# A hybrid RG-LRU / RWKV-7 / PEER layer on one core: norms, LRU chain, picking stage and last rows cut in halves, with more buffers and another order of the one-hot loads

## The reference

```python
h = rms_norm(x, norm1_g)
proj = h @ w_in                                   # 2048 -> LRU branch, gate branch, RWKV columns
# group A: RG-LRU, 1024 channels
a  = exp(-8 * sigmoid(xc @ wa + ba) * softplus(-lam))
bx = sqrt(1 - a * a) * (sigmoid(xc @ wi + bi) * xc)
h_t = a_t * h_(t-1) + bx_t                        # a scan over the 256 tokens
y_lru = h * gelu(gate)
# group B: RWKV-7 time mixing, 16 heads of 64 -> y_rwkv
x = x + concat(y_lru, y_rwkv) @ w_out
# PEER: 8 heads, 128 x 128 single-neuron experts, top 16 of each head
h = rms_norm(x, norm2_g)
q = h @ wq;  scores against 2 x 128 keys;  experts e = 128 * i + j;  g = softmax(best 16)
act = gelu(h . u_tab[e])                          # 128 experts (8 heads x 16) per token
x = x + sum_e  g_e * act_e * v_tab[e]
return rms_norm(x, normf_g)
```

## Time and profile before

| | before |
|---|---|
| median of three executions | 2071.92 us |
| profiled execution | 2072.16 us |
| its span | 2070.4 us |
| mean granted TensorE clock | 0.991 |
| TensorE busy | 1990.3 us (96%) |
| VectorE busy | 1546.8 us (75%) |
| ScalarE busy | 970.3 us (47%) |
| GpSimd busy | 500.9 us (24%) |
| moved by DMA | 462.00 MB, mean 223 GB/s |

### The profile page before, as it was taken

How to read it: one execution, slowest core, us unless ns; L and a number is a source line. 1 busy time by engine, 2 the same in 40 slices (tenths; PEclk the granted TensorE clock), 3 DMA queues, 4 the chain that set the end, 5 groups by cost and what they waited for, 6 DMA issues and landing times.

```text
span 2070.4 us, 35268 instructions
## 1 busy us (share of the span) xinstructions
PE 1990.3 (96%) x14048; PEld 1766.5 (85%) x14048; DVE 1546.8 (75%) x2341; ACT 970.3 (47%) x1332; POOL 500.9 (24%) x513
## 2 busy tenths in 40 slices
PE   7999999898999999999999999998989999999997
PEld 7988888786789888888888888888878888888886
DVE  5647474756453799997867888757778998989998
ACT  5434342436353444444444444445664444444443
POOL 1000000000000000000012222104665766666664
PEclk9999999999999999999999999999999999999999
DMA  7523232224555565656668888866879999999996
GB/s 251 163 73 121 65 123 73 83 89 165 179 189 173 175 187 189 184 186 190 184 223 280 283 289 285 265 192 209 281 232 315 340 341 341 347 349 361 355 353 246
DMA packets 148675, 462.00 MB, mean 223 GB/s; under 512 B 19856, under 2 KB 44480, under 8 KB 147744
## 3 DMA queue, kind: packets, MB, share of 16 engines
q1 hardware_dynamic: 114624, 338.74, 50.4%
q0 software_dynamic: 33888, 121.01, 16.7%
HBM read 430.24 MB, written 29.43 MB: 222 GB/s over the span
## 4 chain that ended last, share of the span: by engine, by line
PE 86%; DVE 6%; DMA 3%; ACT 2%; issue 1%; POOL 0%; DVEq 0%; SPq 0%; POOLq 0%; ACTq 0%
PE ps L1565 86%; DMA oneJ<-oneJ_spill 2%; DVE lo L999 1%; DVE L L1188 1%; ACT hi L658 0%; DVE xc L1007 0%; DMA x_sb<-in_x 0%; DMA vraw<-in_peer_v 0%; ACT x_sq L671 0%; ACT xr_sq L671 0%; DMA got<-in_peer_v,row_ids 0%; ACT lt L831 0%; DVE ps L1485 0%; PE ps L1714 0%; DVE xr L1007 0%
## 5 line engine op out<-in xcount | busy, mean ns | idle before, releaser
L1565 PE MATMUL ps<-hT,hi 128*128 128x512 f32 (+1 forms) x3936 | 1072.6, 345 | 6.3 <-DVE rkv L1007 3.6
L1565 PE MATMUL ps<-hT,lo 128*128 128x256 f32 x2992 | 839.2, 280 | 0.0
L1565 PEld LDWEIGHTS ps<-hT,hi 128*128 128x128 f32 x3936 | 679.8, 190 | 105.2 <-DVE rkv L1007 4.2
L999 DVE TENSOR_TENSOR lo<-raw,hi 128x1024 fp32r<-128x1024 f32 x406 | 492.3, 1224 | 230.6 <-ACT hi L658 224.3
L658 ACT ACTIVATE hi<-raw 128x1024 fp32r<-128x1024 f32 x406 | 424.4, 1059 | 450.2 <-DMA raw<-in_peer_u 371.0
L1565 PEld LDWEIGHTS ps<-hT,lo 128*128 128x128 f32 x2992 | 567.6, 190 | 0.0
L616 POOL DMA_INDIRECT got<-in_peer_v,row_ids x256 | 325.7, 1272 | 174.7 <-DVE sums L1007 116.9
L903 ACT ACTIVATE vhi<-vraw 128x1024 fp32r<-128x1024 f32 (+1 forms) x256 | 202.6, 816 | 272.1 <-DMA vraw<-in_peer_v 267.2
L1467 DVE TENSOR_TENSOR vlo<-vraw,vhi 128x1024 fp32r<-128x1024 f32 (+1 forms) x256 | 240.4, 940 | 52.6 <-ACT vhi L903 45.2
L1565 PE MATMUL ps<-vhi,a_hi 128*128 128x512 f32 (+1 forms) x768 | 252.6, 383 | 2.2 <-ACT wT L930 2.2
L1565 PE MATMUL ps<-vlo,a_hi 128*128 128x512 f32 (+1 forms) x768 | 253.5, 384 | 0.0
(11 more groups left out here) (286 smaller groups left out, 1840.5 us busy)
## 6 DMA issues: line engine op xcount, KB each, us to landing
raw<-in_peer_u SPq DMA_DIRECT2D x256, 512.0 KB, 3.6
vraw<-in_peer_v SPq DMA_DIRECT2D x128, 512.0 KB, 6.3
raw<-in_w_in SPq DMA_DIRECT2D x86, 512.0 KB, 3.6
vraw<-in_peer_v SPq DMA_DIRECT2D x128, 224.0 KB, 6.1
raw<-in_w_out SPq DMA_DIRECT2D x32, 512.0 KB, 3.5
raw<-in_wq SPq DMA_DIRECT2D x32, 512.0 KB, 3.5
oneJ_spill<-madeJ POOLq DMA_DIRECT2D x64, 256.0 KB, 5.0
oneJ<-oneJ_spill SPq DMA_DIRECT2D x64, 256.0 KB, 4.4
```

The costliest lines, as they stand in the source:

```text
L999: V.tensor_tensor(lo[n % NR][:, :], raw[n % NR][:, :], hi[n % NR][:, :].bitcast(F32), ALU.subtract).then_inc(lo_done, 1)
L1565: return nc.tensor.matmul(o, lhsT, rhs, start=start, stop=stop, skip_group_check=True)
```

## The change

It touches five places and leaves the products and their operands as they are.

- First norm: x comes in four loads (t and half of the columns), and VectorE and ScalarE square one half each of every t. Root, reciprocal and diagonal are made for one t at a time. SP also asks for `ident` and `cols`; GpSimd's other constants wait for the first projected piece.
- LRU chain: every full-tile step becomes two half-tile steps (`lru_part`, four channel blocks each), with the `hi`/`lo` pieces of w_out placed between the halves by `hi_out` and `lo_out`.
- Second norm: the last w_out tile is done for t=0 and then for t=1 by TensorE, and the adds (`add_rows`) and norms (`norm_rows`) follow per t.
- Picking stage: S_LAG from 8 to 6; four `oneG` buffers; the gelu and the weight product for two steps at a time; `load_one_j` stands in front of `load_one_i` in each step; the one-hots of VectorE stand in front of `chosen`, and the first four are made before the stage; the last scores are put in place in two parts (`LAST_TOKENS`); the eight early v loads are spread, one in every six steps (`V_FIRST, V_EVERY = 10, 6`).
- Last rows: the running sums start from the columns of x2 that a load brings (`sums_in`), not from a memset; `picked` is done twice at six places; per t there are an add, a sum, a root and a scaling, of which ScalarE takes a part (`scaled_early`), and the last v tile ends t=0 first.

The diff, cut to its core (the instruction lists of ScalarE at the LRU chain mirror those of VectorE):

```diff
-S_LAG = 8
+S_LAG = 6
 BC_TOK = 8
 N_BC = SEQ // BC_TOK
 N_GATHER = 6
 V_RAWS, V_HIS = 4, 3
-V_FIRST = 44
-N_ONEJ, N_ONEI = 4, 10
+V_FIRST, V_EVERY = 10, 6
+N_ONEJ, N_ONEI, N_ONEG = 4, 10, 4
...
-                sync.dma_start(x_sb[:, t], xv[:, t]).then_inc(sem(f"x_in{t}"), 16)
+                for q in range(2):
+                    part = slice(PIECE * q, PIECE * q + PIECE)
+                    sync.dma_start(x_sb[:, t, part], xv[:, t, part]).then_inc(sem(f"x_in{t}_{q}"), 16)
+                if t == 0:
+                    sync.dma_start(ident[:, :], a["consts"][:, 0:P]).then_inc(sem("ident_in"), 16)
+                    sync.dma_start(cols[:, :], a["cols"]).then_inc(sem("cols_in"), 16)
...
-            for s in range(N_TOK4 + S_LAG - 2):
+            for s in range(N_TOK4 + S_LAG - 3):
                 if s == 0:
                     load_one_i(N_FIRST)
                     load_one_i(N_FIRST + 1)
+                if S_LAG - 3 <= s < N_TOK4 + S_LAG - 3:
+                    load_one_j(s - S_LAG + 3)
                 if N_FIRST + 2 <= s + 2 < N_TOK4:
                     load_one_i(s + 2)
-                if s >= S_LAG - 2:
-                    load_one_j(s - S_LAG + 2)
-                if s >= V_FIRST and s < V_FIRST + 2 * V_RAWS:
-                    load_v(s - V_FIRST)
+                if s >= V_FIRST and (s - V_FIRST) % V_EVERY == 0 and s < V_FIRST + 2 * V_RAWS * V_EVERY:
+                    load_v((s - V_FIRST) // V_EVERY)
+            x2_rows = x2_dram.rearrange("p (t d) -> p t d", t=NT2)
+            sync.wait_ge(sem("alo_done"), 5)
+            sync.dma_start(sums[:, :, :], x2_rows[:, :, DD:D]).then_inc(sem("sums_in"), 16)
...
-                pool.wait_ge(sem("w_done"), g // 4 + 1)
-                if g >= 2:
-                    pool.wait_ge(sem("gates_made"), g - 1)
+                pool.wait_ge(sem("w_done"), g // 2 + 1)
+                if g >= N_ONEG:
+                    pool.wait_ge(sem("gates_made"), g - N_ONEG + 1)
                 wait_one_i(pool, g)
                 nc.gpsimd.tensor_tensor(
-                    oneG[g % 2][:, :, :], one_i(g)[:, :, :],
+                    oneG[g % N_ONEG][:, :, :], one_i(g)[:, :, :],
...
+            for t in range(NT2):
+                act.wait_ge(sem(f"x_in{t}_1"), 16)
+                nc.scalar.activation(x_sq[:, t, PIECE:D], x_sb[:, t, PIECE:D], ACT.Square,
+                                     accum_out=ssq8[:, 2 * t + 1:2 * t + 2]).then_inc(
+                    sem("x_squared"), 1)
+                act.wait_ge(sem("row_sum"), t + 1)
+                nc.scalar.activation(sd[:, t:t + 1], ssq[:, t:t + 1], ACT.Sqrt, scale=1.0 / D,
+                                     bias=eps_c).then_inc(sem("row_root"), 1)
...
+            one_hot_jt(1)
+            one_hot_jt(3)
+            scores_in(N_U - 1, LAST_TOKENS[0])
+            wait_read(act, "tile", T_U + N_U - 1)
+            scores_in(N_U - 1, LAST_TOKENS[1])
             for s in range(N_TOK4 + S_LAG + 1):
-                if s % 2 == 0 and s + 1 < N_TOK4:
+                if s % 2 == 0 and N_FIRST <= s + 1 < N_TOK4:
                     one_hot_jt(s + 1)
-                if s % 4 == 1 and 5 <= s <= N_TOK4 + 1:
-                    b = (s - 5) // 4
-                    act.wait_ge(sem("picks_summed"), 4 * b + 4)
-                    nc.scalar.activation(wgt[:, 16 * b:16 * b + 16], wgt[:, 16 * b:16 * b + 16],
+                if s % 2 and 3 <= s <= N_TOK4 + 1:
+                    b = (s - 3) // 2
+                    act.wait_ge(sem("picks_summed"), 2 * b + 2)
+                    nc.scalar.activation(wgt[:, 8 * b:8 * b + 8], wgt[:, 8 * b:8 * b + 8],
                                          ACT.Gelu_apprx_tanh).then_inc(sem("gelu_done"), 1)
                 if s > S_LAG:
                     gates_in(s - S_LAG - 1)
...
+            lo_out(4, 5)
+            for h in range(2):
+                dve.wait_ge(sem("la_lt_done"), h + 1)
+                link(V.tensor_tensor(lru_part(lr, h), lru_part(la, h), lru_part(la, h), ALU.mult))
+                mark(stt(lru_part(lt, h), lru_part(lr, h), 1.0, lru_part(lt, h), ALU.add, ALU.mult),
+                     "om_done", h + 1)
+                lo_out(6 + h, 6 + h)
             for c in range(CT):
                 wait_read(dve, "tile", ORDER.index(("gate", c)))
+            for h in range(2):
+                dve.wait_ge(sem("om_root"), h + 1)
+                link(stt(lru_part(li, h), lru_part(li, h), 0.5, lru_part(lt, h), ALU.mult, ALU.mult))
+                lo_out(8 + 2 * h, 8 + 2 * h)
+                for c in LRU_HALF[h]:
+                    link(V.tensor_tensor_scan(lr[:, c], la[:, c], li[:, c], 0.0, ALU.mult, ALU.add))
+                    if c == LRU_HALF[h][1]:
+                        lo_out(9 + 2 * h, 9 + 2 * h)
+                mark(V.tensor_tensor(lru_part(lt, h), lru_part(lr, h), lru_part(gate, h), ALU.mult),
+                     "yL_f32", h + 1)
+            for h in range(2):
+                lo_out(12 + h, 12 + h)
+                dve.wait_ge(sem("yL_hi"), h + 1)
+                V.tensor_tensor(lru_part(yL_lo, h), lru_part(lt, h), lru_part(yL_hi, h).bitcast(F32),
+                                ALU.subtract).then_inc(sem("yL_lo"), 1)
+            lo_out(14, 2 * N_OUT + 1)
...
+            def add_rows(t, chunks):
+                dve.wait_ge(mm_done, 2 * T_Q) if t else dve.wait_ge(sem("rows_out"), 1)
+                for j in chunks:
+                    xs = x2[:, t, j * 512:(j + 1) * 512]
+                    V.tensor_tensor(xs, xs, bank("out", 4 * t + j), ALU.add).then_inc(
+                        freed("out", 4 * t + j), 1)
+
+
+            add_rows(0, range(4))
+            norm_rows(0)
+            add_rows(1, range(4))
+            norm_rows(1)
...
             one_hot_jt(0)
+            one_hot_jt(2)
+            for n, part in enumerate(LAST_TOKENS):
+                z_add(N_U - 1, part, n)
             for s in range(N_TOK4 + S_LAG):
+                if s % 2 and N_FIRST <= s + 1 < N_TOK4:
+                    one_hot_jt(s + 1)
                 if 1 <= s <= N_TOK4:
                     chosen(s - 1)
-                if s % 2 and s + 1 < N_TOK4:
-                    one_hot_jt(s + 1)
-                if s % 4 == 2 and 6 <= s <= N_TOK4 + 2:
-                    b = (s - 6) // 4
+                if s % 2 == 0 and 4 <= s <= N_TOK4 + 2:
+                    b = (s - 4) // 2
                     dve.wait_ge(sem("gelu_done"), b + 1)
-                    part = slice(16 * b, 16 * b + 16)
+                    part = slice(8 * b, 8 * b + 8)
                     V.tensor_tensor(wgt[:, part], wgt[:, part], idxT[:, 2, part], ALU.mult).then_inc(
                         sem("w_done"), 1)
                 if 1 <= s <= N_TOK4:
                     summed(s - 1)
-                if s >= 66:
-                    v_lo(s - 66)
+                if s >= N_TOK4 + 4:
+                    v_lo(s - N_TOK4 - 4)
...
+            act_lo(0, slice(0, 1), 0)
+            v_lo(2)
+            v_lo(3)
+            for k in range(1, 4):
                 act_lo(0, slice(k, k + 1), k)
             act_lo(1)
+            v_lo(4)
+            v_lo(5)
             dve.wait_ge(sem("wT_in"), 2)
-            dve.wait_ge(sem("alo_done"), 5)
-            mark(V.memset(sums[:, :, :], 0.0), "sums_zero", 1)
+            dve.wait_ge(sem("sums_in"), 16)
+            picks_done = 0
...
+                for _ in range(2 if done % 40 == 39 else 1):
+                    picked(picks_done)
+                    picks_done += 1
...
+            for j in range(3):
+                add_dense(0, j)
+            add_dense(1, 0)
+            row_sum(0)
+            add_dense(1, 1)
+            add_dense(1, 2)
+            row_scale(0)
...
+            n_last = 2 * (T_OUT + N_OUT - 1)
+            pe.wait_ge(lo_done, n_last + 2)
+            for t in range(NT2):
+                ah, al = (x[:, CT - 1, t * P:(t + 1) * P] for x in (yL_hi, yL_lo))
+                for half in range(2):
+                    n = n_last + half
...
+                ins.then_inc(mm_done, 2) if t else ins.then_inc(sem("rows_out"), 1)
```

408 lines of the change are left out of this document (245 added, 163 removed).

## The result

The changed kernel took 2051.02 us at the median of four executions (2048.45 to 2053.10), against 2071.07 us for the kernel before beside it: a ratio of 0.9896 with a 95% interval of 0.9883 to 0.9909.

The account below looks back on a forecast made before the run. TensorE is busy 96% of the span and no product is removed, so only its 80 us idle can be won. 2072.16 - 4.5 - 7.5 - 3.6 - 15 - 3.2 = 2038.4 us; range 2028 to 2056.

Parts of the forecast that it names:

- A: Whole kernel: the forecast case, most picking steps run at 1.79 us; 2038.4 us, own range 2028 to 2047, chance 0.58.
- rival B: Picking: the lock holds from about the first v load, 50 steps at 2.21 us; 2050.4 us, chance 0.27.
- First norm, -4.5: Kernel start: halves squared by both engines let the projection start 4.8 us earlier; -4.5 us, bounds 0 and -6.
- 1.5 us, which I let cost 0.3: First norm: VectorE makes its small constants behind the turning instead of ahead of it; 1.5 us, counted as 0.3.
- LRU chain, -7.5: w_out: lo pieces between half-width chain steps shorten TensorE's waits; 9.2 us available, 1.7 stay; -7.5, bounds -3 and -9.2.
- Second norm, -3.6: Turning of x2: t=0 ends first, so turning starts earlier with half the products; -3.6 us, bounds 0 and -4.5.
- Picking, -15: Picking stage: dense part starts 24.0 us earlier without stalls, less 9 us of stalls; -15, bounds -24 and +37.
- the lock: Picking: VectorE's one-hot waits while GpSimd's back-to-back multiplications run; once late, it meets the next pair again.
- so it is 0.57 us behind: Picking: GpSimd's pair starts 0.57 us after VectorE's one-hot; if VectorE is later than that, the pair goes first.
- the counted 9 us: Picking: stalls allowed for oneI, oneJ and the lock, taken off the 24.0 us gain.
- C, 2090.9: Picking: v loads keep the DMA side full and each of 58 steps costs 2.85 us; 2090.9 us, chance 0.06.
- Last rows, -3.2: Kernel end: t=0 adds hidden, picks end earlier, ScalarE shares scaling; last store 3.2 us earlier, bounds 0 and -5.

Follow-up runs that it names:

- head_spread: Changed kernel with GpSimd's constants loaded singly over more projection pieces and VectorE's constants behind the first lo pieces; 2047.92 us, ratio 0.9885.
- i_before_j: Changed kernel with the load order of the kernel before: oneI in front of oneJ, and oneJ one step later; 2046.61 us, ratio 0.9868.
- plain_onehot: Changed kernel with VectorE's one-hots in the form that also sums its output into a spare column; 2041.61 us, ratio 0.9849.
- pool_after: Changed kernel with GpSimd's pair of multiplications waiting until VectorE has made the one-hot of the same two steps; 2039.42 us, ratio 0.9846.
- v_burst: Changed kernel with the eight early v loads in eight steps from step 44, instead of one in six; 2052.03 us, ratio 0.9893.
- lru_order: Changed kernel with lo pieces 10 to 13 of w_out one place earlier in VectorE's list of the LRU chain; 2050.70 us, ratio 0.9890.

## Why the prediction was right, and where it was not

The time lies in the range and moved the way forecast, 20 us instead of 33.5. The likeliest case (A, 2038.4, own range to 2047) is not what happened; the profile shows rival B (2050.4), for which the range had been made wide enough. That the time is within 1 us of B's number is partly luck: picking gave 4.5 us more than B says, and the stretch behind the first norm and the LRU chain gave 5.0 us less.

- **First norm, -4.5:** right for the start of the projection. Wrong in what was hidden: "1.5 us, which I let cost 0.3" and GpSimd's loads, which were priced at nothing, brought 4.1 us of waits, 3.0 us net with the changes further on (head_spread: 0.8 us of waits in their place). The wait of 1.1 us at 23.90, right behind VectorE's constants (22.53), is most likely theirs; it wasn't tested apart. The bound of 0 had this case in it.
- **LRU chain, -7.5:** the mechanism was right, and the term mis-sized: -5.5. 1.7 us of waits were let stay; 2.9 stayed. With them 8.5 us were to be had, not 9.2.
- **Second norm, -3.6:** right, with -4.7: the turning runs at full pace in both halves (3.84 us for 32, against 9.85 for 64, in which the granted clock was 0.50).
- **Picking, -15:** -7.5. The tail gave 6.3 of 8 us. The start did not come as forecast: the first eight steps took 14.41 us and not 11.65, since the lock and the slow products were taken to be gone there and were not. The step that failed is the choice between A and B, and in it "so it is 0.57 us behind". Where the one-hots go free, as for six of them in i_before_j, the pair is 0.79 us behind, so the walk itself was right; but the changed kernel meets a pair at 1400.12 already, and from then on the pair mostly starts 0.11 us *ahead* of the one-hot or 0.49 us ahead of it. That this keeps itself up is what the section on the lock said it would do. Rival B's place and price were right in kind; its 2.21 us a step is 2.05, because only every second one-hot waits for both multiplications, and the one after it comes late enough to get in between. The waits for `oneI` and `oneJ` in the counted 9 us were nearly nothing in the changed kernel (0.6 us), since longer steps gave the loads time; they came up when the lock was taken away (plain_onehot).
- From the rule of the Trainium skill (SBUF — State Buffer, Who interferes with whom) the prediction had worked out a wait for one multiplication, by which the stage would lose nothing. The traces show waits for one and for two, and pool_after puts the loss at some 10 us. One thing the rule of who comes first doesn't cover: the one-hots at 1408.80 in the changed kernel (2.72 us) and at 1433.25 in i_before_j stand in the record ahead of the pair, by 0.37 and 0.17 us, behind the start of a `jcast` issue of GpSimd, and waited for both multiplications all the same; why is open. The same section counts `tensor_scalar` among the forms with a two-port mode, but not where it also writes out its accumulator. The trace of plain_onehot agrees: 0.735 to 0.746 us in all 30.
- **C, 2090.9:** DMA share 0.86 at 278 GB/s in these steps; no load was late by much. The spread v loads neither cost nor gain at the longer steps (v_burst).
- **Last rows, -3.2:** -2.6. **Dense part, 0:** -1.0; TensorE was idle for 0.35 us in 230. Before, the granted clock was 0.51 from 1548.30 to 1551.70, at the start of this part, and now it is 1.00 there, which fits the 1.0 us.

## What to carry to other kernels

When VectorE and GpSimd work side by side, look in the trace for VectorE instructions that get longer beside GpSimd's (here the one-hot of 0.47 us; `chosen` and the summing form did not), and tie GpSimd's start to their end: one semaphore wait was worth some 10 us, about half of what the whole change brought. An order that just avoids a meeting is one small delay away from the lock (0.35 us in i_before_j), so it needs a semaphore and not a margin. More buffers can cost time: they let an engine bunch its work, and the engine that has to wait for it pays (some 6 us here). A long wait of TensorE can cost twice, by itself and by a lower clock behind it. What is moved from ahead of a stage to behind its start has to be priced as if it stood on the path, until the list of what is due next says otherwise.

## What the runs showed of the hardware

- VectorE's one-hot (128x512, bf16 to f32) takes 0.47 us alone, and up to 2.72 beside GpSimd in the changed kernel. Starting 0.11 us behind a pair of multiplications it waited for both, 0.49 us behind it for one, and 1.02 us behind it for the second one. `chosen`, which reads one operand from PSUM, took 0.684 to 0.690 us in all 56 between 1400 and 1515 us, beside them or not. The form that also sums took 0.735 to 0.746.
- A one-hot that gets in between delays GpSimd too: 2.22 us for the pair in place of 2.05.
- With the same waits of TensorE, the first eight picking steps took 14.41 us where the granted clock fell to 0.50 among them (after) and 12.77 where it stayed at 1.00 (lru_order).
- The same head, in ten profiles, had the projection start between 16.8 and 18.2 us and took 443.9 to 446.7 us from there: a stage's time from a single profile is good to 1 or 2 us where late loads or falls of the clock lie in it (here 3.4 to 10.2 us at the lower level). The stretch without late loads (query projection to first picks) took 817.9 to 818.2 us in all of them.
